# First unit of a fused two-block kernel: order of the input's parts, the squares, the first lo weights and the mean

## The reference

```python
def _rmsnorm(x, g):
    xf = x.astype(jnp.float32)
    y = xf * lax.rsqrt(jnp.mean(xf * xf, axis=-1, keepdims=True) + EPS)
    return (y * g.astype(jnp.float32)).astype(x.dtype)
...
        h = _rmsnorm(x, ln_mix_g[l])
        proj = h @ w_in[l]
        (aq, ak, av, iq, ik, iw, hq, hf, hi, hg, cb, cc, ch, gates) = _split_cols(proj)
        q = _rmsnorm(aq.reshape(b, s, ATTN_HEADS, HEAD_DIM), q_norm_g[l])
        k = _rmsnorm(ak.reshape(b, s, ATTN_KV_GROUPS, HEAD_DIM), k_norm_g[l])
...
        sc = jax.nn.relu(jnp.einsum('bqhd,bsd->bqhs', qi_b, ki))
        sc = jnp.einsum('bqhs,bqh->bqs', sc, wi_b).astype(jnp.float32)
        causal = key_pos[None, :] <= t[:, None]
        sc = jnp.where(causal[None], sc, -jnp.inf)
        _, idx = lax.top_k(sc, n_sel)
```

## Time and profile before

| | us |
|---|---|
| median of 3 runs | 2323.46 |
| lowest and highest | 2322.9 and 2325.31 |
| the profiled execution | 2321.23 |
| its span in the trace | 2319.4 |
| PE busy in it | 2258.9 (97%) |
| DVE, POOL, ACT busy | 1600.3 (69%), 1109.7 (48%), 788.8 (34%) |
| mean granted TensorE clock | 0.993 of full |

### The profile page before, as it was taken

One profiled execution on the slowest core, in us unless ns is written; L12 is line 12 of the kernel. 1 busy time (PEld: TensorE's weight loads), 2 busy tenths in 40 slices (PEclk: granted clock), 3 DMA queues, 4 the chain that ended last, 5 costly groups with the idle time before them and its releaser, 6 DMA issues.

```text
span 2319.4 us, 29282 instructions
## 1 busy us (share of the span) xinstructions
PE 2258.9 (97%) x10866; PEld 1872.5 (81%) x10866; DVE 1600.3 (69%) x1966; ACT 788.8 (34%) x1064; POOL 1109.7 (48%) x853
## 2 busy tenths in 40 slices
PE   7999998999999999999999999899999999999998
PEld 5678887888888899787878888788888887878886
DVE  7899999965677355445586666877777601567777
ACT  4312242022333256313343333444443101444423
POOL 4236653332233156334478888898895432300140
PEclk9999999999999999999999999999999999999999
DMA  4122123432332412434244444744431311341231
GB/s 154 37 82 70 57 98 112 148 142 100 119 118 101 127 56 74 150 131 169 95 150 155 155 154 153 276 172 148 165 135 50 137 46 45 110 133 43 70 109 73
DMA packets 92559, 267.71 MB, mean 115 GB/s; under 512 B 8784, under 2 KB 25304, under 8 KB 87192
## 3 DMA queue, kind: packets, MB, share of 16 engines
q1 hardware_dynamic: 74512, 196.90, 25.1%
q10 hardware_dynamic: 17928, 69.23, 8.3%
HBM read 183.51 MB, written 81.80 MB: 114 GB/s over the span
## 4 chain that ended last, share of the span: by engine, by line
PE 77%; DVE 18%; ACT 2%; issue 1%; DMA 1%; ACTq 0%; POOL 0%; SPq 0%; DVEq 0%; POOLq 0%
PE pair L1103 31%; PE pair L1439 25%; DVE pen L2378 6%; DVE top L2376 6%; PE pair L1596 4%; PE pair L1347 3%; PE pair L1565 2%; PE pair L1274 1%; PE pair L1552 1%; PE pair L1121 1%; PE pair L1325 1%; PE pair L1314 1%; DVE tsp L2641 1%; PE pair L1316 1%; PE pair L1541 1%
## 5 line engine op out<-in xcount | busy, mean ns | idle before, releaser
L1103 PE MATMUL pair<-actA,w_hi 128*128 128x512 f32 x2016 | 625.8, 392 | 9.9 <-ACT stage L1715 7.8
L1103 PEld LDWEIGHTS pair<-actA,w_hi 128*128 128x128 f32 x2016 | 378.0, 189 | 89.5 <-ACT stage L1715 8.2
L1103 PE MATMUL pair<-actA,w_lo 128*128 128x512 f32 x1008 | 393.6, 391 | 0.0
L937 POOL TENSOR_TENSOR pad<-pad 128x1 f32<-128x1 f32 x111 | 33.1, 298 | 717.6 <-PE pair L1103 632.0
L1439 PE MATMUL pair<-tring,wsp 128*128 128x512 f32 x1344 | 308.0, 391 | 6.8 <-DVE tring L2714 5.7
L1439 PEld LDWEIGHTS pair<-tring,wsp 128*128 128x128 f32 x1344 | 253.5, 189 | 61.1 <-issue 7.6
L941 POOL TENSOR_TENSOR w_lo<-raw,w_hi 128x1024 fp32r<-128x1024 f32 (+1 forms) x111 | 255.1, 2298 | 8.9
L1103 PEld LDWEIGHTS pair<-actA,w_lo 128*128 128x128 f32 x1008 | 189.9, 188 | 40.0
L1439 PE MATMUL pair<-tsp,wsp 128*128 128x512 f32 x768 | 184.0, 391 | 4.2 <-DVE tsp L2641 2.1
L2682 DVE TENSOR_TENSOR xB<-pair,xB 128x1024 f32<-128x1024 f32 x112 | 136.4, 1220 | 71.4 <-PE pair L1439 71.2
L2376 DVE MAX8 top<-pen 128x8 f32<-128x384 f32 (+5 forms) x192 | 171.7, 894 | 6.4
(11 more groups left out here) (407 smaller groups left out, 4359.0 us busy)
## 6 DMA issues: line engine op xcount, KB each, us to landing
raw<-w_in SPq DMA_DIRECT2D x80, 512.0 KB, 3.5
wraw<-w_pair SPq DMA_DIRECT2D x32, 1024.0 KB, 7.3
staged<-hid_d SPq DMA_DIRECT2D x56, 512.0 KB, 3.2
proj<-stage ACTq DMA_DIRECT2D x40, 512.0 KB, 2.7
hid_d<-hsum SPq DMA_DIRECT2D x16, 1024.0 KB, 5.0
gates<-proj ACTq DMA_DIRECT2D x24, 512.0 KB, 5.1
raw<-w_out SPq DMA_DIRECT2D x16, 512.0 KB, 3.6
hid_d<-hid SPq DMA_DIRECT2D x16, 512.0 KB, 2.7
```

The lines of the kernel that those rows point to most:

```text
L1103: last = nc.tensor.matmul(pair[par][:, cols], w[:, slot, wk], x[:, cols], start=(k == 0 and i == 0), stop=(k == kt - 1 and i == 2))
```

## The change

Four things, all in the first unit's surroundings:

- SP: the load of unit 1's weights is issued behind x tiles 6 and 7, not ahead of them.
- ACT: hi part of tile 0, square of tile 0, then the hi parts of tiles 1 to 7, then the squares of tiles 1 to 7. DVE: lo part of tile 0, then the lo weights of unit 0 (new there), lo parts of tiles 1 to 7, then the seven sums.
- POOL: makes only the hi weights of unit 0, without the operation on `pad`; then waits for seven lo parts of x (`part_lo`) before it splits unit 1.
- PE: unit 0 is written out: for each k, both halves of w_hi x_hi (waits for the hi part), both of w_hi x_lo (waits for the lo part), both of w_lo x_hi. Then the whole half 0 of unit 1, the mean, and half 1 of unit 1.

```diff
@@ SP
             for j in range(1, NT - 2):
                 load_x(j)
-            sp.dma_start(raw[:, 1, :], t["w_in"][1]).then_inc(w_in[1], 16)
             load_x(NT - 2)
             load_x(NT - 1)
+            sp.dma_start(raw[:, 1, :], t["w_in"][1]).then_inc(w_in[1], 16)
@@ POOL
-            split_units(0, 1, 8)
+            pool.wait_ge(w_in[0], 16)
+            nc.gpsimd.tensor_copy(w_hi[:, 0, :], raw[:, 0, :]).then_inc(w_hi_ok, 1)
+            pool.wait_ge(part_lo, NT - 1)
             split_units(1, 1, 8)
@@ PE
-            product_first(0, 8, hX, lX, part_lo, 0)
-            product(1, 1, 0, 8, hX, lX, (0,), (0, 1))
+            pe.wait_ge(w_hi_ok, 1)
+            for k in range(8):
+                wk = slice(k * P, (k + 1) * P)
+                for m, (w, x) in enumerate(((w_hi, hX(k)), (w_hi, lX(k)), (w_lo, hX(k)))):
+                    if m == 0:
+                        pe.wait_ge(raw_hi, k + 1)
+                    elif m == 1:
+                        pe.wait_ge(part_lo, k + 1)
+                    elif k == 0:
+                        pe.wait_ge(w_split, 1)
+                    for half in range(2):
+                        cols = slice(half * HALF, (half + 1) * HALF)
+                        mm = nc.tensor.matmul(pair[0][:, cols], w[:, 0, wk], x[:, cols],
+                                              start=(k == 0 and m == 0), stop=(k == 7 and m == 2))
+            mm.then_inc(unit_mm, 1)
+            product(1, 1, 0, 8, hX, lX, (0,))
             pe.wait_ge(x_in, 48)
             pe.wait_ge(squares_used, NT - 1)
...
             mm.then_inc(squares_used, 1)
-            product(1, 1, 0, 8, hX, lX, (0,), tuple(range(2, 8)))
             product(1, 1, 0, 8, hX, lX, (1,))
@@ ACT
                 nc.scalar.activation(rawx[:, j, 0, :], X0[:, j, :], ACT.Copy, scale=SM("ln_mix", j)).then_inc(raw_hi, 1)
+                if j == 0:
+                    nc.scalar.activation(rstd[:, :], X0[:, 0, :], ACT.Square).then_inc(squares, 1)
+            for j in range(1, NT):
                 if j >= 3:
                     act.wait_ge(squares_used, j - 2)
-                nc.scalar.activation(xsq[(j - 1) % 2][:, :] if j else rstd[:, :], X0[:, j, :], ACT.Square) \
-                  .then_inc(squares, 1)
+                nc.scalar.activation(xsq[(j - 1) % 2][:, :], X0[:, j, :], ACT.Square).then_inc(squares, 1)
@@ DVE
-                if j:
-                    dve.wait_ge(squares, j + 1)
-                    if j > 1:
-                        dve.wait_ge(squares_used, j - 1)
-                    V.tensor_tensor(rstd[:, :], rstd[:, :], xsq[(j - 1) % 2][:, :], ALU.add).then_inc(squares_used, 1)
+                if j == 0:
+                    dve.wait_ge(w_hi_ok, 1)
+                    V.tensor_tensor(w_lo[:, 0, :], raw[:, 0, :], w_hi[:, 0, :].bitcast(F32), ALU.subtract) \
+                     .then_inc(w_split, 1)
+            for j in range(1, NT):
+                dve.wait_ge(squares, j + 1)
+                if j > 1:
+                    dve.wait_ge(squares_used, j - 1)
+                V.tensor_tensor(rstd[:, :], rstd[:, :], xsq[(j - 1) % 2][:, :], ALU.add).then_inc(squares_used, 1)
```

## The result

| | before | after |
|---|---|---|
| median of 9 runs, us | 2323.46 | 2328.97 |
| lowest and highest | 2321.67 and 2326.52 | 2326.45 and 2331.73 |
| span of the profiled execution | 2319.4 | 2327.2 |
| unit 0 over on PE | 30.57 | 21.24 |
| last sum of squares over | 29.98 | 32.6 |

The changed kernel is **slower** by 0.2%: ratio 1.0022, interval 1.0013 to 1.0031. Unit 0 did end 9.3 us earlier, and yet everything that hangs on the mean came later.

What follows compares the result with a forecast made beforehand. DVE's row was taken to bound the start, delaying PE, the chain behind 401 us. Terms 0.8 - 0.3 + 0 + 1.5 = +2.0 us on 2323.46 gave 2325.5, range 2320.5 to 2328.3.

Steps and rivals of the forecast that it cites:

- three signs that were to show it wrong: Sums ending before 30 us, unit 4's split holding no low_x, or the stall at 393 changing length.
- slack before 401: PE's stall at 393 to 401: PE alone has 7.81 us to spare against DVE, so the start counts through DVE.
- rival D: Clock falls before the mean: its records take 3.4 us instead of 1.7, +1.7; whole sum +5.4, 2328.8; chance 0.12.
- a slow start behind its idle time: Half 0 of unit 1: some 7.1 us with 8 matmuls at half clock, against 5.45 warm, ending at 30.5 to 30.9.
- the 9.4 us: Unit 0 on PE ends 9.4 us earlier; this becomes PE idle time before unit 1, the mean and the scores.
- the 1.55 of the sum: First score operation, held 1.98 against 0.43 before: a hold of 1.55 us that goes when unit 4's split moves.
- the 2.14 of before: Unit 3's split behind the mean: its subtraction held DVE by 2.14 us before; kept the same, so term 0.
- -0.3: Ahead of take(2): take(1) and take(2) no longer wait for PE, so the 0.28 us gap goes.
- 3.05: Unit 4's split among low_x and scale_x ahead of take(2): costs a whole split, given as 2.95 to 3.1 us.
- +0.8: Start of the mean: two splits hold the sums, so it starts at 32.5 us, not 31.77.
- +1.5: Unit 4's split: holds low_x and scale_x for 2.95 to 3.1 us, where it held a score operation for 1.55.
- The 3.39: A weight split's cost to DVE by the exclusive lock rule: cast 1.03 plus subtraction 2.36 us.

Runs made afterwards that it cites:

- e5: Changed kernel with 28 unread matmuls more behind the first two pieces of unit 3, ahead of the first score products; median 2328.74 us, ratio 1.0019.
- e6: Changed kernel with GpSimd splitting unit 2 only behind the sums and unit 4 only beside take(2); median 2323.02 us, ratio 0.9997.
- e8: Changed kernel with unit 2's split behind the sums, unit 4's beside take(2), and 16 matmuls more before the first score product; median 2323.02 us, ratio 0.9995.
- e3: Changed kernel with GpSimd splitting unit 4 only when scaling 6 is done, beside take(2); median 2327.41 us, ratio 1.0015.
- e11: Changed kernel with GpSimd making only 1 of the 1024 columns of unit 3's lo weights (result not the reference's); 2323.31 us, one run.
- e1: Changed kernel with 14 unread matmuls more between half 0 of unit 1 and the mean; median 2328.88 us, ratio 1.0021.
- e4: Changed kernel with squares and sums back between the hi and lo parts, as in the kernel before; median 2332.67 us, ratio 1.0037.
- e9: Changed kernel with sums back between the lo parts and the mean directly behind unit 0, ahead of all of unit 1; median 2321.57 us, ratio 0.9987.
- e10: As e9, but ScalarE makes unit 1's hi weights and VectorE its lo weights, so GpSimd splits nothing before unit 2; median 2321.82 us, ratio 0.9986.

## Why the prediction was wrong

The time lies above the range's end, 2328.3, and the forecast of no change stood at 0.88, slower at 0.08. None of the three signs that were to show it wrong came (the sums did not end before 30 us, unit 4's split did hold a lo part, the stall kept its length): it failed where it had set no sign.

**What held.** That DVE's row decides and TensorE has slack before 401: the stall stayed 7.81, and the shift at the landmark is that at the piece. Unit 0 was over near 21 (21.24), the lo weights of unit 1 came at 23.4 (20.21 + 3.20), the last sum ended at 32.6 (32.5 foreseen), and the mean started right behind it at 32.75. The turns of cast, sum, subtraction, sum were those read off, twice over. The end of the sums is right in part by luck: free sums follow each other at 1.24 to 1.33 us, as the chain above shows, and not at 1.17, and a split cost them 2.75 and not 2.95 to 3.3. A detail differs: the first cast did not wait for lo part 0 but held it (2.15 instead of 1.28 us), so PE began at 7.43 and not at 8.4. And the splits of units 3 and 4 moved 1.3 us ahead, not 3.5, since the slow mean kept half 1 of unit 1 back.

**The first step that failed** is the choice between the forecast and rival D. The forecast took the mean at the full clock, since only 1.6 us of idle time stood before it; the gap was 3.55, because half 0 of unit 1 ended at 29.2 and not at 30.5 to 30.9. I had charged unit 1 a slow start behind its idle time (2.21 us) that it did not have, and so the gap went to the mean, where it was not wanted. (In e5, e6 and e8, with gaps of 2.93 to 3.03 us there, unit 1 did run slow in part, and the mean was fast.) D's price was right: +1.7 predicted, +1.68 measured. I had given it 0.12. Even D's whole sum, +5.4, falls short of the 6.8 measured, and that is the second step.

**The second** is the sentence that the 9.4 us become idle time of PE "before the scores", as if that were free. It cost the low clock in the stretch from 62.2 to 65.2. The prediction has no term for it. The stage from take(2) to the piece grew by 0.72 + 0.28 although the first score operation was held no more: by e5, the low clock cost 2.16, and the hold that went away gave back 1.16, not the 1.55 of the sum. Rows for it were at hand: the low clock behind 3.19 idle us in the earlier trace rows, and 57 against 51.5 in my own numbers for take(2) and the end of unit 2, a gap of over 5 us.

**The third** is a size: unit 3's split costs 2.97 (2.06 and 3.41 against 1.28 and 1.22) where I kept the 2.14 of before, its cast being no longer free, and unit 4's costs 2.70 ahead of take(2). Together with the 0.28 that went away this is 2.97 - 2.14 + 2.70 - 0.28 = 3.25 against 3.18 measured; the prediction's terms ahead of take(2) were -0.3, 0 and 3.05, 2.75 together, and behind it the 1.55 of the held score operation were to be saved, where 1.0 was added. All terms: +0.8, -0.3, 0 and +1.5 were predicted, 2.0; +0.98 (mean's start), +1.68 (its clock), +3.18 (take(0) to take(2)) and +1.0 (scores) were measured, 6.8.

The Trainium skill's rule of the exclusive lock (SBUF — State Buffer, section "Who interferes with whom") agrees with the rows here: the sums of 2.02 and 3.2 were held 0.8 and 2.0 us, nearly the length of a cast (1.04) and of a subtraction (2.4), and the scaling took 1.22 where the subtraction was cut to one column. The 3.39 that the prediction worked out by that rule for a split lay nearer to the 2.97 of unit 3 than the 2.14 that I kept.

The description of the kernel before says that 12 matmuls of unit 1 stood ahead of the mean; they were 6. The prediction's sum did not use it, since it took the end of half 0 from unit 1's weights on, but it hid that the move costs 4.1 us where nothing else gives way.

**What stays open**: when the clock goes down. Behind the same idle time of 4.36 us it was down from the first score product on in e6 (1.00 us) and only some 0.4 us later in e3 (0.67, and 0.84 for the next). Behind 2.93 to 3.03 us it fell about 1 us into unit 1 in e5, e6 and e8, and behind 3.00 us it did not fall at the scores of e11. The mean was slow behind 3.5 us (three executions) and fast behind 1.91, 0.76 and 0.34. How many executions have which, no run here tells; the medians of e1 and e5, 0.2 and 1.3 us better than the changed kernel's against their own befores, say that filling the gaps gains less on average than in the traces. And of the 7.8 us between the two spans some 1 us arose behind the landmark, where I have no experiment.

## What to carry to other kernels

An engine that is made faster ahead of a wait is only an idle engine, and here TensorE paid for being idle with its clock, at the very instructions on which the others wait: look at what runs first behind each new gap, and whether it is on the path. When work on one engine moves in time, list the other engine's long operations that will now fall beside it: here four holds of 0.8 to 2.2 us each, behind the mean alone, came from GpSimd's splits, which no line of the DVE program names. And put the short instruction that releases a long row (the mean) as soon as its own inputs are there, ahead of the matmuls that merely fill time.

## What was not expected of the hardware

GpSimd does not always get its turn. Between the seven sums of the changed kernel it got it after every one; beside the scalings a cast stood 2 us longer (the cast of 3.24 at 44.26) and held nobody. I took this for a matter of DVE's waits, since each sum waits for a semaphore and a scaling for nothing, but the rows of e4 speak against it: its last sum waits for semaphores too and took 1.23, while GpSimd's cast stood. What decides the turn is open.

```profile
23.64 3.24 POOL L939 CAST w_hi<-raw 128x1024 fp32r<-128x1024 f32 x1
```

A DVE operation with one input in PSUM was not held and held nobody: take(2) took 1.22 or 1.23 us before and in e3, e6, e8, e9 and e10, with a cast of 1.04 or 1.05 beside it.

The cost of a delay was not its length. Removing a hold of 2.2 us brought the landmark 6.16 us forward, and moving the mean by 4.1 us moved it by 7.5, through later holds and the clock.
